# Two transformer blocks on one core: the FFNs' middle layers and u moved within 64 bytes

## The chip, the core and the metric

The kernel runs on one core of a Trainium2 chip. The metric is the device time of one execution in microseconds (us); of several executions the median is taken. The engines are TensorE (PE; its weight loads have a row of their own, PEld), VectorE (DVE), ScalarE (ACT), GpSimd (POOL) and SyncE (SP), which here issues the loads of the weights.

## The reference

Two blocks in a row on 256 tokens of 1024 features, in float32. The first block is an FFN, a mixer (gated linear attention and block attention), and an FFN; the second is the same frame twice (layers 1 and 2) with another mixer. Each FFN has a middle layer of 2816 features:

```
def swiglu(x, w_gate, w_up, w_down):
    return (jax.nn.silu(x @ w_gate) * (x @ w_up)) @ w_down

first block:   h = h + FFN_RES * g1 * swiglu(u, w_ff1_gate, w_ff1_up, w_ff1_down)   # u: normalised h
               h = h + g2 * token_mixing(u, w_in, ...)
               h = h + FFN_RES * g3 * swiglu(u, w_ff2_gate, w_ff2_up, w_ff2_down)
second block:  for l in range(2): the same order with swiglu_2 and concat(conv, hgrn2, fox) mixers
```

So there are six FFNs, numbered 0 to 5, and three mixers, numbered 0 to 2.

## The kernel before

Features lie on the 128 partitions and tokens along the free dimension, so a tile is 128 features by 256 tokens. u (the normalised input of a projection) has KD = 8 such tiles, an FFN's middle layer KF = 22. Float32 products are made of three matmuls in a rounded format: the weights and the moving operand are each split into a high and a low part (whi, wlo; uhi, ulo; hhi, hlo; mix_hi, mix_lo), and `three` (line 1749) issues high by high, high weights by low, low weights by high, each with 128 x 128 weights and a moving operand of 128 x 256. One such group is called a triple here.

Stages follow in this order: up0, down0, in0, branch, out0, up1, down1, up2, down2, in1, out1, up3, down3, up4, down4, in2, out2, up5, down5. An up projection has 22 chunks of weights, each of two halves (gate and up) by 8 tiles k: 352 triples, 1056 matmuls (`feature_tiles`, `first_tiles` for the chunk that waits for u). A down projection has 16 chunks of 11 tiles of the middle layer: 176 triples, 528 matmuls (`down` in TensorE's `ffn`). Chunks come by DMA into `raw`, a ring of 4 slots. ScalarE rounds a chunk into whi (line 750), VectorE subtracts into wlo (lines 1064 and 1073), and TensorE waits for wlo (`chunk_in`). PSUM banks alternate. The order of the work is written out by hand, with semaphores between engines.

Beside that, ScalarE writes a tile of uhi (line 798, or 777 for up0 and part of in0), VectorE writes ulo (lines 1099, 1115); ScalarE writes a tile of hhi (lines 819 and 829), VectorE writes hlo from it (line 1307).

Where the operands stand, in bytes along a partition. Tensors are placed one behind the other in the order in which they are declared, rounded up to 32 bytes. In the built program whi begins at 49280, wlo at 82048, ulo at 131200, uhi_room at 139392, mix_lo at 151808, hhi_room and merged_a at 180864, mix_hi at 184960 and merged_b at 203392: all are multiples of 64. hlo_room begins at 203424, 32 bytes past a multiple of 64. The slots of whi and wlo are 8192 bytes apart, weights within a slot step by 512 bytes, and tiles of the moving operands by 1024 bytes, so every tile of an operand has its first tile's place within 64 bytes, with one exception. `ahead = 8` elements of 4 bytes put uhi and hhi 32 bytes into their rooms:

```
        ahead = 8
        uhi_room = sb("uhi_room", [P, ahead + KD * (T + 2)], F32R)
        uhi = uhi_room[:, ahead:ahead + KD * T].rearrange("p (k t) -> p k t", t=T)
        uhi_shift = uhi_room[:, ahead:].rearrange("p (k t) -> p k t", t=T + 2)
```

The exception is uhi_shift, used in up1 and in the first two chunks of in0 (`shift_tiles`, `shift_three`, `second_of_in0`). There the high part has 258 columns per tile, two more than the 256 tokens, and tiles step by 1032 bytes, so tile k stands 32 + 8k bytes past a multiple of 64. In `second_of_in0` each k serves two triples in a row. In in0 from its third chunk on, and in in1 and in2, `token_tiles` uses the parts of u as the weights for some chunks and whi, wlo as the moving operand.

hhi_room and hlo_room share their bytes with tensors of the mixers (lv, aq, ak, av, gat and others down to cross). hidden_end only reserves the end of that overlap; prob and prob_t stand behind it.

Of the kernel before, what the change touches and what calls it, by code (L numbers as in the profile page):

```python
# [23 lines left out]
P = 128  # L24
T = 256
# [33 lines left out]
IN_CHUNKS = [GLA_CHUNKS, MIX_CHUNKS, MIX_CHUNKS]  # L59
ATT_HEADS = [4, 8, 8]  # L60
# [108 lines left out]
def build(nc, a, out):  # L169
    with ExitStack() as ctx:  # L170
# [21 lines left out]
        uhi = uhi_room[:, ahead:ahead + KD * T].rearrange("p (k t) -> p k t", t=T)  # L192
        uhi_shift = uhi_room[:, ahead:].rearrange("p (k t) -> p k t", t=T + 2)
        uhi_shifted = uhi_shift[:, :, 0:T]
# [71 lines left out]
        hhi_room = hidden.enter_context(nc.sbuf_tensor("hhi_room", [P, ahead + KF * T], F32R))  # L266
        hlo_room = hidden.enter_context(nc.sbuf_tensor("hlo_room", [P, KF * T], F32R))
        hhi = hhi_room[:, ahead:].rearrange("p (k t) -> p k t", t=T)
        hlo = hlo_room[:].rearrange("p (k t) -> p k t", t=T)
# [24 lines left out]
        sb("hidden_end", [P, 2 * KF])  # L294
# [447 lines left out]
        def _(act):  # L742
# [65 lines left out]
            def ffn(i):  # L808
                n0, e0 = seg(f"up{i}")

                def step(t, it=0):
                    dst = tiles_of(hhi, t, it, RING)
# [28 lines left out]
                def down(t):  # L841
                    split_ahead(n0 + t)
                    if t % 2 and name:
                        if g is not None:
                            if i == 0 and t == 1:
                                act.wait_ge(mods, 2)
                            gained_hi(g, e0 + t // 2, t // 2, into=uhi if i else uhi_shifted)
                        else:
                            act.wait_ge(evacuated, 2 + e0 + t // 2 + 1)
# [54 lines left out]
            def mixer(m):  # L904
# [100 lines left out]
                for t in range(4):  # L1005
# [3 lines left out]
                    for k in (2 * t, 2 * t + 1):  # L1009
                        gained_hi(g, e0 + t, k, into=uhi if m else uhi_shifted)  # L1010
# [47 lines left out]
        def _(dve):  # L1058
# [212 lines left out]
            def ffn(i, first_scale=None):  # L1271
                n0, e0 = seg(f"up{i}")

                def step(t, it=0):
# [32 lines left out]
                    nc.vector.tensor_tensor(tiles_of(hlo, t, it, RING), src, tiles_of(hhi, t, it, RING).bitcast(F32),  # L1307
# [35 lines left out]
                def down(t, it=0):  # L1343
# [4 lines left out]
                    else:  # L1348
# [16 lines left out]
                        if after is not None:  # L1365
                            gained_lo(SPLITS.index(FOLLOWS[f"down{i}"]), after, m, it, 2, uhi if i else uhi_shifted)
# [193 lines left out]
            def mixer(m):  # L1560
# [110 lines left out]
                for t in range(4):  # L1671
# [12 lines left out]
                    for k in (2 * t, 2 * t + 1):  # L1684
                        gained_lo(SPLITS.index(FOLLOWS[f"out{m}"]), next_gain(f"out{m}"), k, hi=uhi if m else uhi_shifted)
# [60 lines left out]
        def _(pe):  # L1746
# [14 lines left out]
            def feature_tiles(n, dst, tiles, width, kt):  # L1761

                vh, vl = kview(whi, n % RING, KD, width), kview(wlo, n % RING, KD, width)
                for j in tiles:
                    c = slice(j * P, (j + 1) * P)
                    for k in range(kt):
                        ins = three(dst[:, j * T:(j + 1) * T], vh[:, k, c], vl[:, k, c], uhi[:, k], ulo[:, k],
# [3 lines left out]
            def first_tiles(n, dst, waits, parted=(KD - 2, None)):  # L1771
# [3 lines left out]
                for ks in (range(at), range(at, KD)):  # L1775
                    if between and ks[0]:
                        between()
                    for j in range(2):
                        c = slice(j * P, (j + 1) * P)
                        for k in ks:  # L1780
                            if j == 0:
                                pe.wait_ge(ulo_ready, waits + k + 1)
                            ins = three(dst[:, j * T:(j + 1) * T], vh[:, k, c], vl[:, k, c], uhi[:, k], ulo[:, k],
# [136 lines left out]
            def ffn(i, stats=None):  # L1920

                n0, e0 = seg(f"up{i}")
                waits = KD * SPLITS.index(f"up{i}")

# [364 lines left out]
```

## Time and profile before

| | |
|---|---|
| time, median of 3 runs | 1637.3 us (1635.99 to 1637.68) |
| the profiled execution: its own time | 1638.61 us |
| its span | 1636.9 us |
| mean granted clock of TensorE | 0.999 |
| matmuls in the trace | 13617 |
| bytes read from HBM | 313.04 MB, 192 GB/s over the span |

The span runs from the first to the last instruction. The granted clock is a share of 2.4 GHz: 1.00 is the upper level and 0.50 the lower, 1.2 GHz. A matmul's displayed duration overlaps with that of the next ones, and so does a weight load's. How fast they follow each other is read from their starts, or from how many there are in a window. In a window that is filled from end to end, PE busy equals its length. The count in a window holds each instruction of which any part falls into it.

### The profile page before, as it was taken

To read this page: it belongs to the slowest core of one execution; us is meant where nothing else is said; L and a number is where in the kernel's file an instruction comes from. 1 tells how busy PE (TensorE), PEld (TensorE's weight loads), DVE (VectorE), ACT (ScalarE), POOL (GpSimd) and SP (SyncE) were. 2 spreads that over 40 slices of the span, in tenths; PEclk is the share of its full clock that TensorE was granted. 3 is DMA by queue.
4 is the path that set the end of the run, shared out by engine and by line. 5 is a ranking of instruction groups with operands and counts; after the bars stand their busy time and mean duration, and the time that the engine had idled before them with its cause. 6 is when DMAs were issued, how large, how long until landed. Compare 5 with 4: busy or idle time off the path is not lost.

```text
span 1636.9 us, 33817 instructions
## 1 busy us (share of the span) xinstructions
PE 1613.2 (99%) x13617; PEld 1575.4 (96%) x13617; DVE 1154.4 (71%) x1452; ACT 800.5 (49%) x973; POOL 171.6 (10%) x193
## 2 busy tenths in 40 slices
PE   6999999999999999999999999999999999999999
PEld 4999999999999999999999999999999999999999
DVE  6877789778766657666688876656665588776653
ACT  3444445355544455444464654445444465564442
POOL 1100114500000000000052200000000035200000
PEclk9999999999999999999999999999999999999999
DMA  9998797645766477655744566568664764456653
GB/s 332 312 313 248 243 333 228 219 153 182 183 188 187 133 196 205 193 165 159 230 140 130 146 179 189 150 178 218 192 189 142 209 190 130 129 157 190 177 160 114
DMA packets 501553, 315.62 MB, mean 193 GB/s; under 512 B 14815, under 2 KB 489674, under 8 KB 501450
## 3 DMA queue, kind: packets, MB, share of 16 engines
q1 hardware_dynamic: 491824, 282.33, 60.4%
q0 software_dynamic: 8496, 29.92, 5.2%
q8 instruction: 76, 1.25, 0.3%
q10 hardware_dynamic: 1130, 1.90, 0.3%
q14 instruction: 27, 0.22, 0.0%
HBM read 313.04 MB, written 1.05 MB: 192 GB/s over the span
## 4 chain that ended last, share of the span: by engine, by line
PE 71%; DVE 4%; ACT 2%; issue 1%; ACTq 0%; DVEq 0%
PE accs L1751 20%; PE accs L1753 20%; PE accs L1752 19%; PE accs L1789 1%; PE wide L1789 1%; PE wide L1791 1%; PE accs L1791 1%; PE wide L1790 1%; PE accs L1790 1%; DVE wlo L1064 1%; PE wide L2022 1%; PE accs L1849 1%; PE accs L1850 0%; PE accs L1851 0%; PE ps_score L2071 0%
## 5 line engine op out<-in xcount | busy, mean ns | idle before, releaser
L1751 PE MATMUL accs<-uhi_room,whi 128*128 128x256 f32 x2304 | 651.7, 283 | 3.0 <-DVE ulo L1115 1.2
L1753 PE MATMUL accs<-uhi_room,wlo 128*128 128x256 f32 x2304 | 646.4, 281 | 0.0
L1752 PE MATMUL accs<-ulo,whi 128*128 128x256 f32 x2304 | 644.3, 280 | 0.0
L750 ACT CAST whi<-raw 128x2048 fp32r<-128x2048 f32 (+2 forms) x294 | 500.5, 1705 | 107.1 <-PE accs L1753 60.7
L1064 DVE TENSOR_TENSOR wlo<-raw,whi 128x2048 fp32r<-128x2048 f32 (+2 forms) x249 | 496.5, 2002 | 4.5 <-ACT gat L991 3.1
L1751 PEld LDWEIGHTS accs<-uhi_room,whi 128*128 128x128 f32 x2304 | 435.6, 189 | 11.4 <-issue 5.2
L1752 PEld LDWEIGHTS accs<-ulo,whi 128*128 128x128 f32 x2304 | 432.1, 188 | 1.2 <-issue 1.2
L1753 PEld LDWEIGHTS accs<-uhi_room,wlo 128*128 128x128 f32 x2304 | 433.1, 188 | 0.0
L1751 PE MATMUL accs<-hhi_room,whi 128*128 128x256 f32 x1056 | 296.3, 281 | 0.8 <-DVE wlo L1064 0.8
L1752 PE MATMUL accs<-hlo_room,whi 128*128 128x256 f32 x1056 | 295.2, 280 | 0.0
L1753 PE MATMUL accs<-hhi_room,wlo 128*128 128x256 f32 x1056 | 294.4, 279 | 0.0
L1751 PEld LDWEIGHTS accs<-hhi_room,whi 128*128 128x128 f32 x1056 | 198.4, 188 | 2.0 <-issue 1.7
L1753 PEld LDWEIGHTS accs<-hhi_room,wlo 128*128 128x128 f32 x1056 | 198.5, 188 | 0.0
L1752 PEld LDWEIGHTS accs<-hlo_room,whi 128*128 128x128 f32 x1056 | 198.5, 188 | 0.0
L824 ACT ACTIVATE work<-work 128x256 f32<-128x256 f32 x88 | 37.0, 420 | 217.7 <-DVE work L1293 217.7
L1293 DVE TENSOR_TENSOR work<-accs,rstd 128x512 f32<-128x512 f32 x99 | 68.4, 691 | 103.7 <-PE accs L1753 103.5
L1073 DVE TENSOR_TENSOR wlo<-raw,whi 128x1024 fp32r<-128x1024 f32 (+1 forms) x90 | 116.2, 1296 | 0.5
L1307 DVE TENSOR_TENSOR hlo_room<-work,hhi_room 128x256 f32 (+1 forms) x132 | 56.2, 425 | 84.9 <-ACT hhi_room L829 77.8
L1363 DVE SCALAR_TENSOR_TENSOR h<-accs,half,h 128x256 f32 (+1 forms) x48 | 23.2, 484 | 114.3 <-PE accs L1753 114.3
L829 ACT CAST hhi_room<-work 128x256 f32 (+1 forms) x110 | 44.8, 407 | 42.7 <-DVE work L1303 35.1
L639 POOL DMA_DIRECT2D in_turn<-in_w_ada x56 | 30.3, 541 | 272.8 <-DVE intra L1240 153.8
L798 ACT ACTIVATE uhi_room<-h,vec_b 128x256 fp32r<-128x256 f32 x40 | 19.6, 509 | 79.3 <-DVE h L1363 66.3
(368 smaller groups left out, 2263.8 us busy)
## 6 DMA issues: line engine op xcount, KB each, us to landing
raw<-in_ffn_w_in SPq DMA_DIRECT2D x176, 512.0 KB, 5.0
in_turn<-in_w_ada POOLq DMA_DIRECT2D x56, 512.0 KB, 5.6
raw<-in_w_mix_in SPq DMA_DIRECT2D x52, 512.0 KB, 4.6
raw<-in_ffn_w_out SPq DMA_DIRECT2D x64, 384.0 KB, 3.6
raw<-in_w_ff_gate SPq DMA_DIRECT2D x44, 512.0 KB, 5.0
raw<-in_w_ff_up SPq DMA_DIRECT2D x44, 512.0 KB, 6.2
raw<-in_w_in SPq DMA_DIRECT2D x40, 512.0 KB, 5.1
raw<-in_ffn_w_out SPq DMA_DIRECT2D x64, 320.0 KB, 4.0
```

What stands on the lines that cost most here:

```text
L750: nc.scalar.copy(whi[:, n % RING, 0:cols], raw[:, n % RING, 0:cols]).then_inc(hi_ready, 1)
L824: nc.scalar.activation(pair[:, 0], pair[:, 0], ACT.Silu, bias=ws[:, t % 2, 0:1] if i == 1 else 0.0).then_inc(silu_ready, 1)
L829: nc.scalar.copy(dst, pair[:, 1]).then_inc(hhi_ready, 1)
L1064: nc.vector.tensor_tensor(wlo[:, n % RING, 0:cols], raw[:, n % RING, 0:cols], whi[:, n % RING, 0:cols].bitcast(F32), ALU.subtract).then_in ...
L1073: ins = nc.vector.tensor_tensor(wlo[:, n % RING, c], raw[:, n % RING, c], whi[:, n % RING, c].bitcast(F32), ALU.subtract)
L1293: nc.vector.tensor_tensor(pair, ps, by_token(2), ALU.mult).then_inc(evacuated, 1)
L1307: nc.vector.tensor_tensor(tiles_of(hlo, t, it, RING), src, tiles_of(hhi, t, it, RING).bitcast(F32), ALU.subtract).then_inc(hlo_ready, 1)
L1751: mm(dst, wh, xh, start=first, stop=False)
L1752: mm(dst, wh, xl, start=False, stop=False)
L1753: return mm(dst, wl, xh, start=False, stop=last)
L1789: mm(dst, wh, uhi_shift[:, k], start=first, stop=False)
L1790: mm(dst[:, 0:T], wh, ulo[:, k], start=False, stop=False)
```

## The change

Each of the six FFNs gets a place of its own for its middle layer, for hhi and hlo alike: `MIDDLE_FROM` elements into the rooms, which are 16, 48, 40, 24, 56 and 8 bytes for FFN 0 to 5. hhi_room is larger, so that hlo_room begins at 203648, now a multiple of 64. uhi begins at 16, 48, 40 and 24 bytes for up2, up3, up4 and up5, and stays at 32 for up0, in1, in2 and the later chunks of in0; up1 and the first chunks of in0 keep uhi_shift. ulo stays. The order of the instructions on each engine is the same, and so are their number and shapes; the parameters that carry the tiles (`xh`, `hhi[i]`) only choose addresses. prob and prob_t stand 128 bytes further up.

```diff
 IN_CHUNKS = [GLA_CHUNKS, MIX_CHUNKS, MIX_CHUNKS]
+MIDDLE_FROM = [4, 12, 10, 6, 14, 2]
 ATT_HEADS = [4, 8, 8]
...
         uhi_room = sb("uhi_room", [P, ahead + KD * (T + 2)], F32R)
-        uhi = uhi_room[:, ahead:ahead + KD * T].rearrange("p (k t) -> p k t", t=T)
+        def uhi_from(c):
+            return uhi_room[:, c:c + KD * T].rearrange("p (k t) -> p k t", t=T)
+
+        uhi = uhi_from(ahead)
         uhi_shift = uhi_room[:, ahead:].rearrange("p (k t) -> p k t", t=T + 2)
-        uhi_shifted = uhi_shift[:, :, 0:T]
+        uhi_of = {"in0": uhi_shift[:, :, 0:T], "up1": uhi_shift[:, :, 0:T], "up2": uhi_from(4), "in1": uhi, "up3": uhi_from(12),
+                  "up4": uhi_from(10), "in2": uhi, "up5": uhi_from(6)}
         work = sb("work", [P, 4, T])
...
         hidden = ExitStack()
-        hhi_room = hidden.enter_context(nc.sbuf_tensor("hhi_room", [P, ahead + KF * T], F32R))
-        hlo_room = hidden.enter_context(nc.sbuf_tensor("hlo_room", [P, KF * T], F32R))
-        hhi = hhi_room[:, ahead:].rearrange("p (k t) -> p k t", t=T)
-        hlo = hlo_room[:].rearrange("p (k t) -> p k t", t=T)
+        hhi_room = hidden.enter_context(nc.sbuf_tensor("hhi_room", [P, KF * T + 8 * ahead], F32R))
+        hlo_room = hidden.enter_context(nc.sbuf_tensor("hlo_room", [P, KF * T + 2 * ahead], F32R))
+        hhi, hlo = [[room[:, c:c + KF * T].rearrange("p (k t) -> p k t", t=T) for c in MIDDLE_FROM]
+                    for room in (hhi_room, hlo_room)]
         hidden.close()
...
         cross = sb("cross", [P, 4, P])
-        sb("hidden_end", [P, 2 * KF])
+        sb("hidden_end", [P, 80])
         prob = sb("prob", [P, 384])
...
                 def step(t, it=0):
-                    dst = tiles_of(hhi, t, it, RING)
+                    dst = tiles_of(hhi[i], t, it, RING)
                     if i == 0:
...
                                 act.wait_ge(mods, 2)
-                            gained_hi(g, e0 + t // 2, t // 2, into=uhi if i else uhi_shifted)
+                            gained_hi(g, e0 + t // 2, t // 2, into=uhi_of[FOLLOWS[f"down{i}"]])
                         else:
...
                     for k in (2 * t, 2 * t + 1):
-                        gained_hi(g, e0 + t, k, into=uhi if m else uhi_shifted)
+                        gained_hi(g, e0 + t, k, into=uhi_of[FOLLOWS[f"out{m}"]])
                     square_pair(["up1", "up3", "up5"][m], t)
...
                     src = hid[:, t % 2] if i == 0 else gate_up[:, t % 2, 1]
-                    nc.vector.tensor_tensor(tiles_of(hlo, t, it, RING), src, tiles_of(hhi, t, it, RING).bitcast(F32),
+                    nc.vector.tensor_tensor(tiles_of(hlo[i], t, it, RING), src, tiles_of(hhi[i], t, it, RING).bitcast(F32),
                                             ALU.subtract).then_inc(hlo_ready, 1)
...
                         if after is not None:
-                            gained_lo(SPLITS.index(FOLLOWS[f"down{i}"]), after, m, it, 2, uhi if i else uhi_shifted)
+                            gained_lo(SPLITS.index(FOLLOWS[f"down{i}"]), after, m, it, 2, uhi_of[FOLLOWS[f"down{i}"]])
                         split_ahead(n0 + t, it)
...
                     for k in (2 * t, 2 * t + 1):
-                        gained_lo(SPLITS.index(FOLLOWS[f"out{m}"]), next_gain(f"out{m}"), k, hi=uhi if m else uhi_shifted)
+                        gained_lo(SPLITS.index(FOLLOWS[f"out{m}"]), next_gain(f"out{m}"), k, hi=uhi_of[FOLLOWS[f"out{m}"]])
                     if t == 0 and m:
...
-            def feature_tiles(n, dst, tiles, width, kt):
+            def feature_tiles(n, dst, tiles, width, kt, xh=uhi):
                     for k in range(kt):
-                        ins = three(dst[:, j * T:(j + 1) * T], vh[:, k, c], vl[:, k, c], uhi[:, k], ulo[:, k],
+                        ins = three(dst[:, j * T:(j + 1) * T], vh[:, k, c], vl[:, k, c], xh[:, k], ulo[:, k],
                                     k == 0, k == kt - 1)
-            def first_tiles(n, dst, waits, parted=(KD - 2, None)):
+            def first_tiles(n, dst, waits, parted=(KD - 2, None), xh=uhi):
...
                                 pe.wait_ge(ulo_ready, waits + k + 1)
-                            ins = three(dst[:, j * T:(j + 1) * T], vh[:, k, c], vl[:, k, c], uhi[:, k], ulo[:, k],
+                            ins = three(dst[:, j * T:(j + 1) * T], vh[:, k, c], vl[:, k, c], xh[:, k], ulo[:, k],
                                         j == 0 and k == 0, j == 1 and k == KD - 1)
...
                 waits = KD * SPLITS.index(f"up{i}")
+                xh = uhi_of[f"up{i}"] if i else uhi
...
                     elif t == 0 and isinstance(it, int):
-                        ins = first_tiles(n0, acc[e0 % 2], waits, (4, second_part) if i == 0 else (KD - 2, None))
+                        ins = first_tiles(n0, acc[e0 % 2], waits, (4, second_part) if i == 0 else (KD - 2, None), xh)
                     elif i == 0 and t == 1 and isinstance(it, int):
                     else:
-                        ins = feature_tiles(n0 + t, acc[(e0 + t) % 2], range(2), 2 * P, KD)
+                        ins = feature_tiles(n0 + t, acc[(e0 + t) % 2], range(2), 2 * P, KD, xh)
                     ins.then_inc(chunk_used, 1)
...
                         kk = side * (KF // 2) + k
-                        ins = three(acc[(e0 + m) % 2][:, 0:T], vh[:, k], vl[:, k], hhi[:, kk], hlo[:, kk],
+                        ins = three(acc[(e0 + m) % 2][:, 0:T], vh[:, k], vl[:, k], hhi[i][:, kk], hlo[i][:, kk],
                                     kk == 0, kk == KF - 1)
```

## Rows read from the trace of the kernel before

**Rows 1.** The page: busy time of each engine, and the chain's shares by engine.

```profile
PE 1613.2 (99%) x13617; PEld 1575.4 (96%) x13617; DVE 1154.4 (71%) x1452; ACT 800.5 (49%) x973; POOL 171.6 (10%) x193
...
PE 71%; DVE 4%; ACT 2%; issue 1%; ACTq 0%; DVEq 0%
```

**Rows 2.** Matmuls in order of time, out0: start us, length us, engine, line.

```profile
412.00 0.28 PE L1751 MATMUL accs<-merged_a,whi 128*128 128x256 f32 x1
...
415.36 0.28 PE L1752 MATMUL accs<-merged_b,whi 128*128 128x256 f32 x1
```

**Rows 3.** Stretches: window, length, PE busy (matmuls), clock, DMA share, GB/s.

```profile
648.00:738.00 90.00, 90.00 (x766) 1.00 0.65 182
172.00:187.00 15.00, 15.00 (x131) 1.00 0.62 191
216.00:234.00 18.00, 18.00 (x155) 1.00 0.93 311
574.00:614.00 40.00, 40.00 (x345) 1.00 0.70 195
764.00:804.00 40.00, 40.00 (x342) 1.00 0.70 202
1080.00:1120.00 40.00, 40.00 (x342) 1.00 0.69 198
1268.00:1308.00 40.00, 40.00 (x345) 1.00 0.71 205
450.00:540.00 90.00, 90.00 (x754) 1.00 0.67 182
```

**Rows 4.** The stretch of half clock in in0, as rows 3, and its matmuls: start, length.

```profile
249.00:249.80 0.80, 0.80 (x6) 0.50 1.11 356
...
248.70 0.42 PE L1789 MATMUL wide<-uhi_room,whi 128*128 128x258 f32 x1
...
249.77 0.42 PE L1791 MATMUL wide<-uhi_room,wlo 128*128 128x258 f32 x1
```

**Rows 5.** Matmuls in order of time, out2, same columns.

```profile
1430.82 0.28 PE L1751 MATMUL accs<-mix_hi,whi 128*128 128x256 f32 x1
...
1434.36 0.27 PE L1751 MATMUL accs<-mix_hi,whi 128*128 128x256 f32 x1
```

**Rows 6.** Matmuls in order of time, one tour of up1.

```profile
496.15 0.28 PE L1789 MATMUL wide<-uhi_room,whi 128*128 128x258 f32 x1
...
496.87 0.28 PE L1789 MATMUL wide<-uhi_room,whi 128*128 128x258 f32 x1
...
497.22 0.28 PE L1789 MATMUL wide<-uhi_room,whi 128*128 128x258 f32 x1
...
497.58 0.28 PE L1789 MATMUL wide<-uhi_room,whi 128*128 128x258 f32 x1
...
497.94 0.29 PE L1789 MATMUL wide<-uhi_room,whi 128*128 128x258 f32 x1
...
498.31 0.28 PE L1789 MATMUL wide<-uhi_room,whi 128*128 128x258 f32 x1
...
499.03 0.28 PE L1789 MATMUL wide<-uhi_room,whi 128*128 128x258 f32 x1
```

**Rows 7.** Matmuls in order of time, second chunk of in0.

```profile
254.61 0.28 PE L1789 MATMUL wide<-uhi_room,whi 128*128 128x258 f32 x1
...
256.03 0.28 PE L1789 MATMUL wide<-uhi_room,whi 128*128 128x258 f32 x1
```

**Rows 8.** Writes of uhi and hlo: count, ns least/median/most, first and last start.

```profile
L798 ACT ACTIVATE uhi_room<-h,vec_b x40: 495/511/514, 757.6 to 1447.9; 128x256 fp32r<-128x256 f32 x40
...
L798 ACT ACTIVATE uhi_room<-h,gain x16: 495/510/513, 179.6 to 434.4; 128x256 fp32r<-128x256 f32 x16
...
L829 ACT CAST hhi_room<-work x110: 397/407/410, 444.2 to 1572.7; 128x256 f32 x80, 128x256 fp32r<-128x256 f32 x30
...
L1307 DVE TENSOR_TENSOR hlo_room<-work,hhi_room x132: 416/426/427, 55.5 to 1573.1; 128x256 f32 x76, 128x256 fp32r<-128x256 f32 x56
```

## The prediction, made before the change was run

> **What bounds the kernel now.** I read the page's first part, then its chain of waits, then steady stretches one by one, single matmuls in order of time, and last the writes of the operands. The first part is to show that TensorE is occupied in 1613.2 of 1636.9 us at the full granted clock, VectorE in 71% [rows 1]. The chain says the same from the other end: 71% of what led to the last instruction is TensorE and only 4% VectorE [rows 1]. So what moves the time is the spacing of matmuls, not their displayed duration. Single matmuls are shown 0.28 us long [rows 2], which holds their time in the pipeline, and they overlap: in 90 us of the third FFN's up projection (up2) there are 766 of them [rows 3]. As each is shown some 280 ns long at a spacing near 118 ns, a window counts about 280 / 118 = 2.4 that began before it; 90 us / (766 - 2.4) = 117.9 ns. That is how I read a spacing from every row of group 3.
>
> For one stretch the granted clock was 0.50, which is 1.2 GHz: five matmuls from 248.70 to 249.77, 214 ns each, or 256 columns at 1.2 GHz to within 1 ns [rows 4]. At 2.4 GHz the same would be 107 ns, so at the full level some 11 ns per matmul are lost that are not lost at the half level. Nothing in the trace waits in these stretches (PE busy equals the window in every row of group 3), so the 11 ns lie inside TensorE, and the reads of the weights and of the moving operand are what is left. Addresses could matter there, and they are all that the change touches. That the reads are the cause is my guess; no row shows it.
>
> **What the spacings say about addresses.** All rooms start at multiples of 64 bytes except hlo_room, which starts 32 bytes behind one. So before the change the offsets within 64 bytes are: weights 0, ulo 0, uhi 32, hhi 32, hlo 32, merged_a, merged_b, mix_hi and mix_lo 0. From the rows:
> - uhi 32 with ulo 0 (up2 to up5): 90 / 763.6 = 117.9 ns [rows 3]; up3 to up5 count 766 or 767 in windows of the same length, so I use 117.8.
> - hhi 32 with hlo 32 (the down projections): 345 in 40 us gives 40 / 342.6 = 116.8, 342 gives 40 / 339.6 = 117.8 [rows 3]. Down1 and down4 run at 116.8 (and down5, whose window of 40 us counts 345 too), down2 and down3 at 117.8, with the very same addresses of the operands. Down0 begins at 15 / 128.6 = 116.6 and ends at 18 / 152.6 = 118.0. So there are two levels for one layout, 1.0 to 1.1 ns apart, and something other than the offset chooses.
> - merged, all at 0: 28 matmuls from 412.00 to 415.36, 120.0 ns [rows 2].
> - mix, all at 0 too: 30 matmuls from 1430.82 to 1434.36, 118.0 ns [rows 5]. So the offset within 64 bytes is not the whole story either: 0 gives 120.0 in one place and 118.0 in another.
> - up1, where uhi steps by 258 elements, so that its offset goes through 32, 40, 48, 56, 0, 8, 16, 24 as k rises: 90 / 751.6 = 119.7 ns [rows 3]; one tour of eight k, 24 matmuls from 496.15 to 499.03, 120.0 [rows 6]. Two of three matmuls have 258 columns here; two columns at 2.4 GHz are 0.8 ns, 0.6 on the mean. That leaves 119.2, or 1.4 ns above the fixed offset of 32.
> - the same layout in in0's second chunk, where two triples in a row have the same offset: 12 matmuls from 254.61 to 256.03 (offsets 8, 16, 16, 24), 118.3 ns [rows 7], 117.7 without the two columns. Here odd offsets cost nothing. So the 1.4 ns of up1 may belong to the change of offset at every k, not to the offsets.
>
> **The change part by part.** (1) Up projections 2 to 5: uhi goes from 32 to 16, 48, 40 and 24 bytes, ulo stays at 0. 4 x 1056 = 4224 matmuls. (2) Down projections: hhi and hlo go to 16, 48, 40, 24, 56 and 8 bytes, from 32 both. 6 x 528 = 3168 matmuls. hlo_room begins at a multiple of 64 bytes now, and lies 224 bytes further up. (3) Up0, in0, up1, in1, in2, out and branch keep their operands' addresses. (4) The instructions that write uhi, ulo, hhi and hlo write or read shifted addresses: cast 407 ns, VectorE's subtraction 426 ns [rows 8]. The 16 activations of line 798 that take their scale from gain write uhi for in0 and up1, all at the touring offsets, in 495 to 513 ns with a median of 510; the 40 that take it from vec_b write at 32 and have a median of 511 [rows 8], so a shifted write costs nothing, and VectorE and ScalarE have slack (busy in 71% and 49% of the span) to hide it if it did. If that cover were gone, the spread of the cast, 397 to 410 ns, times 22 tiles would be 0.3 us per FFN. (5) hidden_end grows, which moves prob and prob_t by 128 bytes, by whole blocks of 64. I take 0.
>
> No row of before shows parts (1) and (2) at a fixed offset of 16, 48, 40, 24, 56 or 8 for long. Bounds from the nearest rows: below, every triple at 116.7 as down4: up 4224 x 1.1 = 4.6 us, down2, down3 and half of down0 1320 x 1.1 = 1.5 us, 6.1 us gained. Above, every triple at 120.0 as merged: 4224 x 2.2 = 9.3 us, and down from a mean of 117.2 3168 x 2.8 = 8.9 us, 18.2 us lost. The nearest row is the chunk of in0 with held offsets, at 117.7: I take 117.8 for up, that is 0. For down I take the mean over the two levels, 117.2, as it is: 0. Sum 0 for the whole kernel. The profiled execution took 1638.6 us around its span of 1636.9; the three timed runs have a median of 1637.3, 1.3 below it, and the prediction is for such a median: 1637.3 us.
>
> The Trainium skill's page "SBUF — State Buffer", section "Specifications (TRN2)", says that SBUF has 16-byte cachelines and that each crossing to a new line costs a penalty. By that rule 40, 24, 56 and 8 bytes would be worse than 16, 32 and 48, since 1024 bytes then touch 65 lines. The held offsets of 8 and 24 in group 7 don't show it; I keep it as a rival below.
>
> **The rivals.** (A) Faster. If what costs is that the moving read and the weight read start in the same place of a block, any offset but 0 is free: hi at 32 gives 116.7 for two matmuls and ulo at 0 gives 120.0 for the third, mean 117.8, as measured in up; merged 120.0 fits, down4's 116.7 fits. Then down2, down3 and late down0 should have been at 116.7 too, and mix at 120.0: against it. With offsets that suit better than 32 both levels can fall: in up1 the triple at 48 is the shortest of the tour, 496.87 to 497.22 or 350 ns, with 258 columns [rows 6]. The bound below prices it: 1637.3 - 6.1 = 1631.2. It counts as faster from 3.3 us (0.2% of 1637, about the least that a measurement of this kernel tells from no change), that is 0.45 ns over 7392 matmuls.
> (B) Slower. 32 is half a block, the furthest from every boundary, and each other offset is nearer to one; up1's 119.2 is then the price of an average offset. 4224 x 1.4 = 5.9 and 3168 x 2.0 = 6.3 us: 12.2 us, 1649.5. If half of the groups pay, 1643.4. For it: the longest triple of the tour is the one at 8, 497.94 to 498.31 or 370 ns, behind 360 at 0 [rows 6]. Against it: group 7. It decides from 0.45 ns on the mean.
 Against it group 7 and up1's tour, where the odd multiples of 8 take 0.35 to 0.37 us like the even ones.
> (D) The layout does not do what it says, as writes at shifted places become slow enough to reach TensorE: with the spread of the cast, 13 ns, for each of 132 tiles all on the path that is 1.7 us, 1639.0.
>
> **How the numbers follow.** No change in sum (a few offsets better, a few worse, within 3.3 us): 0.44. A 0.24, B 0.23, C 0.06, D 0.03, of which D mostly stays within 0.2%. So faster 0.24, within 0.2% 0.45, slower 0.31. The likeliest case's own range is 1634 to 1640.6. Stretched towards A's end (1631) and to B's half case with room for some more (1646), leaving out B's full case and the tail above: 1631 to 1646.
>
> **What the changed profile would show.** The same windows over up2 to up5 and down0 to down5, shifted by what was won or lost: counts of 766 in 90 us and 342 to 345 in 40 us for no change; 774 and 345 for A; 757 and 338 for B. Under C down2 to down5 lose and down0, down1 do not. Up1, the in, out and branch stages are controls, to stay within 0.2 us each, in0 and all before it too. The busy times and groups of VectorE and ScalarE should stay within 1%. What makes the prediction wrong: a mean spacing that moves by more than 0.45 ns over the ten groups, in particular if a fixed offset of 16 or 48 locks at 120.0 as merged does, or below 116.

## The result: slower by 0.6%

| | before | changed |
|---|---|---|
| median of 5 runs | 1637.68 us (1635.99 to 1641.24) | 1646.81 us (1645.66 to 1648.48) |
| ratio | | 1.0057, 95% interval 1.0044 to 1.0069 |
| span of the profiled execution | 1636.9 us | 1644.0 us |

The prediction said 1637.3 us, 1631 to 1646, and gave "slower" 0.31. The change is slower, and the time lies 0.8 us above the range. The spans of the two traces differ by 7.0 us. The medians differ by 9.1 us, because the traced execution of the changed kernel (1645.66 us) lies 1.15 us under its median and that of before (1638.61 us) 0.93 us over its own. The kernel before, timed again beside the later kernels, mostly took 1635 to 1638 us at a mean granted clock of 1.000 and 1639.5 to 1642.5 at 0.998 or less, with medians from 1637.7 to 1640.1, so totals that differ by 2 us say little and the stage lengths decide.

The page of the changed kernel, engine by engine, and the shares of the chain (the work that ended last, followed back from the end), against [rows 1]:

```profile
PE 1620.0 (99%) x13617; PEld 1582.9 (96%) x13617; DVE 1154.4 (70%) x1452; ACT 799.7 (49%) x973; POOL 171.5 (10%) x193
...
PE 72%; DVE 4%; ACT 2%; issue 1%; ACTq 0%; DVEq 0%
```

VectorE and ScalarE do what they did (1154.4 and 799.7 us busy, against 1154.4 and 800.5); TensorE has 6.8 us more. The same steady stretches as [rows 3], shifted a little where the stages moved; columns as there:

```profile
650.00:740.00 90.00, 90.00 (x759) 1.00 0.63 177
963.00:1053.00 90.00, 90.00 (x767) 1.00 0.66 183
1150.00:1240.00 90.00, 90.00 (x762) 1.00 0.65 181
1468.00:1558.00 90.00, 90.00 (x757) 1.00 0.65 181
172.00:187.00 15.00, 15.00 (x130) 1.00 0.61 180
217.00:232.00 15.00, 15.00 (x129) 1.00 0.96 319
575.00:615.00 40.00, 40.00 (x340) 1.00 0.68 191
768.00:808.00 40.00, 40.00 (x338) 1.00 0.70 201
1082.00:1122.00 40.00, 40.00 (x335) 1.00 0.70 193
1272.00:1312.00 40.00, 40.00 (x341) 1.00 0.71 200
1588.00:1628.00 40.00, 40.00 (x343) 1.00 0.57 161
450.00:540.00 90.00, 90.00 (x754) 1.00 0.66 181
```

The first four are up2 to up5. Up2 counts 759 matmuls in 90 us, not 766: 118.9 ns instead of 117.9. Up3 counts 767 as before, up4 762, up5 757. The down projections count 335 to 343 in 40 us, against 342 to 345. Down3, now at 24 bytes, is the worst at 335, which is 120.0 ns; down0's two windows give 117.6 and 118.5 ns. Up1, the last row, counts 754 in both. The clock is 1.00 in all rows. PE busy equals the window in all, but as each matmul is shown some 280 ns long, a short wait would not show in it. The starts in the traces tell more: there is one gap of 203 ns in the window at 172 and one in that at 1588, with 202 ns at the same places before, and no gap over 135 ns in the other rows.

By stage, from the start of a stage's first matmul to that of the next stage's (us), and the mean distance of successive starts in it (ns, gaps over 160 ns left out), worked out from the two traces:

| stage, its offset in bytes | before | changed | ns before | ns changed |
|---|---|---|---|---|
| down0, 32 to 16 | 67.36 | 67.13 | 116.9 | 118.2 |
| down1, 32 to 48 | 62.83 | 63.59 | 116.7 | 118.4 |
| up2, uhi 32 to 16 | 126.76 | 127.76 | 117.8 | 118.9 |
| down2, 32 to 40 | 62.18 | 62.99 | 117.8 | 119.3 |
| up3, uhi 32 to 48 | 125.27 | 125.27 | 117.8 | 117.8 |
| down3, 32 to 24 | 62.18 | 63.37 | 117.8 | 120.0 |
| up4, uhi 32 to 40 | 125.25 | 126.02 | 117.8 | 118.5 |
| down4, 32 to 56 | 61.64 | 62.30 | 116.8 | 118.0 |
| up5, uhi 32 to 24 | 125.28 | 126.81 | 117.8 | 119.2 |
| down5, 32 to 8 | 61.44 | 62.03 | 116.6 | 117.7 |
| up0, up1, branch, out0 to out2, in1, in2 | | | the same | the same to 0.1 |

The ups lose 3.3 us, the downs 3.8. Down0's slower matmuls don't show in its length, as it waited less. In0 behind it is 0.5 us shorter and the stretch ahead of up0 0.5 longer. In0 says nothing about the offsets: in the eight kernels with the same places in in0 (before, changed, and six below) it took 147.4 to 149.0 us. The stages of the last row kept their lengths within 0.02 us. An entry of the table is a mean over a stage, and a stage can change its spacing on the way: down0 before stood at 116.6 or so until its middle and at 117.8 from there on. The writes of the operands, as in [rows 8]:

```profile
L803 ACT ACTIVATE uhi_room<-h,vec_b x40: 492/511/517, 759.2 to 1452.8; 128x256 fp32r<-128x256 f32 x40
```
```profile
L834 ACT CAST hhi_room<-work x110: 394/407/409, 443.9 to 1579.1; 128x256 f32 x80, 128x256 fp32r<-128x256 f32 x30
```

The medians are 511 and 407 ns, as before.

### The profile page after: what moved, and what is told of

Read it like the earlier page. It is cut to its first block, busy times and chain, and to the rows that moved or that the text cites. A ratio compares the mean times of both kernels' runs of the same rounds, so it can differ in the third digit from the quotient of the medians.

```text
span 1644.0 us, 33772 instructions
## 1 busy us (share of the span) xinstructions
PE 1620.0 (99%) x13617; PEld 1582.9 (96%) x13617; DVE 1154.4 (70%) x1452; ACT 799.7 (49%) x973; POOL 171.5 (10%) x193
## 4 chain that ended last, share of the span: by engine, by line
PE 72%; DVE 4%; ACT 2%; issue 1%; ACTq 0%; DVEq 0%
PE accs L1756 20%; PE accs L1758 20%; PE accs L1757 19%; PE accs L1794 1%; PE wide L1794 1%; PE wide L1796 1%; PE accs L1796 1%; PE wide L1795 1%; PE accs L1795 1%; DVE wlo L1069 1%; PE wide L2028 1%; PE accs L1854 1%; PE accs L1855 0%; PE accs L1856 0%; PE ps_score L2077 0%
## 5 line engine op out<-in xcount | busy, mean ns | idle before, releaser
L1368 DVE SCALAR_TENSOR_TENSOR h<-accs,half,h 128x256 f32 (+1 forms) x48 | 23.2, 484 | 118.8 <-PE accs L1758 118.7
```

## The experiments

"Distance" below is how many bytes an operand starts behind the place of the weights, within 256 bytes. Spacings are means of successive starts as in the table, unless a row is named.

**Which part costs.** First the two halves of the change apart. Only the middle layers moved:

```diff
-        uhi_of = {... "up2": uhi_from(4), ... "up3": uhi_from(12), "up4": uhi_from(10), ... "up5": uhi_from(6)}
+        uhi_of = {... "up2": uhi_from(8), ... "up3": uhi_from(8), "up4": uhi_from(8), ... "up5": uhi_from(8)}
```

> Only the middle layers are moved (hhi and hlo at 16, 48, 40, 24, 56, 8 bytes, hlo_room 224 bytes up); uhi stays at 32 in every up projection. Theory (each stage has its own price, set by its own operands' addresses, and nothing else changes): up2 to up5 return to 126.8, 125.3, 125.3 and 125.3 us, the down projections stay as changed, 63.6, 63.0, 63.4, 62.3, 62.0 for down1 to down5, and the time is 3.3 us under the changed kernel's, 3.8 over the kernel before. Rival (the levels pass on from stage to stage): the downs change as well when the ups before them do.

Measured: 1642.19 us, ratio to before 1.0026 (1.0014 to 1.0038). In order up2, up3, down2, down3:

```profile
650.00:740.00 90.00, 90.00 (x766) 1.00 0.65 180
963.00:1053.00 90.00, 90.00 (x767) 1.00 0.64 180
768.00:808.00 40.00, 40.00 (x337) 1.00 0.71 205
1082.00:1122.00 40.00, 40.00 (x336) 1.00 0.68 191
```

The ups are back at 766 and 767, the downs at 337 and 336. Down1, down2, down3 take 63.60, 62.98, 63.37 us, as in the changed kernel to 0.01 us, and down5 62.02; down4 took 62.42, not 62.30.

Only u moved, rooms and middle layers as before:

```diff
-MIDDLE_FROM = [4, 12, 10, 6, 14, 2]
+MIDDLE_FROM = [8, 8, 8, 8, 8, 8]      # no longer read: hhi and hlo and their rooms as in the kernel before
```

> Only u is moved (uhi at 16, 48, 40, 24 bytes in up2 to up5); the middle layers and their rooms are as before. Own-price theory: up2 +1.0, up3 0.0, up4 +0.8, up5 +1.5 us, the downs as before (62.8, 62.2, 62.2, 61.6, 61.4 for down1 to down5), in all +3.3 us over before. Rival (levels pass on): the downs behind a changed up get another of the two levels seen before, 61.6 or 62.2 us.

Measured: 1641.42 us, 1.0016 (1.0005 to 1.0027). The same four windows:

```profile
650.00:740.00 90.00, 90.00 (x759) 1.00 0.64 179
963.00:1053.00 90.00, 90.00 (x762) 1.00 0.65 182
768.00:808.00 40.00, 40.00 (x345) 1.00 0.72 208
1082.00:1122.00 40.00, 40.00 (x345) 1.00 0.71 199
```

Up2 759 as in the changed kernel; up3 took 125.99 us here (762, 118.5 ns), where the changed kernel took 125.27 with the same addresses. So 48 has two levels as 32 has, 117.8 and 118.5. The downs were all at 345 (116.7 ns), down2 and down3 too. A stage has its own price, but which of its levels it gets differs between executions of nearly the same program.

**Offset or distance between the parts.** The change also put hlo_room 224 bytes further up. With the rooms of the changed kernel and 8 elements ahead everywhere, and with the changed offsets in one room that keeps hlo 22528 bytes behind hhi:

```diff
-        hhi_room = ...; hlo_room = ...
+        both_room = hidden.enter_context(nc.sbuf_tensor("both_room", [P, 2 * KF * T + 2 * ahead], F32R))
+        hhi, hlo = [[both_room[:, s + c:s + c + KF * T].rearrange("p (k t) -> p k t", t=T) for c in MIDDLE_FROM]
+                    for s in (0, KF * T)]
```

> The rooms are as changed, but every middle layer starts 8 elements (32 bytes) into them, so within 64 bytes all is as before and only the distance from hhi to hlo grows from 22528 to 22784 bytes, from 44 times 512 to 44.5 times 512. u as before. Theory O (the offset within 64 bytes is what costs): the downs are at 116.7 or 117.8 ns per matmul, as before. Theory D (the distance between the high and the low part, or to the weights, by more than 64 bytes is what costs): the downs are 1.2 to 2.2 ns slower, about 0.6 to 1.2 us each, 3.8 us in all.

> The middle layers start at 16, 48, 40, 24, 56 and 8 bytes past a multiple of 64 as changed, but hhi and hlo lie in one room 22528 bytes apart, as before. u as before. Theory O: the downs cost as in the changed kernel, 3.8 us over before. Theory D: they are as before. If both matter, both this one and the one with only the rooms changed lose a part.

Measured: rooms only 1638.58 us, 1.0004 (0.9994 to 1.0014), down1 to down5 63.34, 62.19, 61.68, 62.19, 61.44 us, at 117.7 or 116.7 ns; that is before's pair of levels. Offsets only 1642.58 us, 1.0030 (1.0019 to 1.0041), down1 to down4 63.59, 62.99, 63.37, 62.42 us. Down2 and down3 with the rooms only, then with the offsets only:

```profile
768.00:808.00 40.00, 40.00 (x342) 1.00 0.71 206
1082.00:1122.00 40.00, 40.00 (x345) 1.00 0.72 200
```
```profile
768.00:808.00 40.00, 40.00 (x338) 1.00 0.70 202
1082.00:1122.00 40.00, 40.00 (x336) 1.00 0.68 191
```

342 and 345 against 338 and 336: the offset costs, and 256 bytes more between the two parts do not. Other distances between them come further down. Down5, at 8 bytes, took 63.02 us (119.6 ns) here and 62.02 in the kernel with only the middle layers moved: so 8 has more than one level. By the starts, the first 12 of its 16 chunks stood at 120.0 ns here and at 117.7 there.

**Does the price belong to the offset?** The same offsets dealt to other FFNs:

```diff
-MIDDLE_FROM = [4, 12, 10, 6, 14, 2]
+MIDDLE_FROM = [2, 14, 6, 10, 12, 4]       # and uhi_from(6), (10), (12), (4) for up2 to up5
```

> The changed kernel with its offsets dealt to other FFNs: hhi and hlo at 8, 56, 24, 40, 48, 16 bytes for FFN 0 to 5, uhi at 24, 40, 48, 16 for up2 to up5. Theory (the price belongs to the offset): down2 at 24 and down3 at 40 swap their 120.0 and 119.3 ns, down4 at 48 takes 118.4, down1 at 56 118.0 to 118.2; up2 at 24 takes 119.2, up3 at 40 118.5, up4 at 48 117.8 or 118.5, up5 at 16 118.9. Rival (the price belongs to the place in the program): each stage keeps the figure of the changed kernel.

Measured, one execution: 1646.05 us. Down2 and down3:

```profile
768.00:808.00 40.00, 40.00 (x336) 1.00 0.69 197
1082.00:1122.00 40.00, 40.00 (x338) 1.00 0.68 188
```

They swapped: 24 bytes gives 120.0 ns wherever it is, 40 gives 119.3; 48 gave 118.3 in down4, 56 118.2 in down1, 16 118.4 in down5. Up2 at 24 took 119.3, up3 at 40 118.5, up4 at 48 117.8. Up5 at 16 took 118.5, not 118.9.

**All at zero.**

```diff
-MIDDLE_FROM = [4, 12, 10, 6, 14, 2]
+MIDDLE_FROM = [0, 0, 0, 0, 0, 0]          # and uhi_from(0) for up2 to up5
```

> The changed kernel with every offset at 0: hhi, hlo and the uhi of up2 to up5 at multiples of 64, like the weights. Theory (0 collides with the weights): 120.0 ns as in out0, ups 127.6 instead of 125.3 us, downs 63.4 instead of 61.6 to 62.2, in all 15 us or more over the kernel before, more than the changed kernel loses. Rival (mix operands stand at 0 and run at 117.8 ns): ups and downs at 117.8, within 2 us of before.

Measured: 1654.28 us, 1.0088 (1.0073 to 1.0104). Up2 and down2, 752 in 90 us and 336 in 40, both 120.0 ns:

```profile
650.00:740.00 90.00, 90.00 (x752) 1.00 0.63 176
768.00:808.00 40.00, 40.00 (x336) 1.00 0.68 197
```

So 32 was indeed better than 0, and mix at 117.8 with offsets of 0 within 64 bytes had to have another reason.

**Relative to what, and with which period.** Two kernels that move more than the change did. The first puts ulo 32 bytes up in a room 64 bytes larger, which moves all that lies behind by 64, hhi and hlo and merged among it. The second moves whi and wlo by 32 and all behind them by 64:

```diff
-        ulo = sb("ulo", [P, KD, T], F32R)
+        ulo_room = sb("ulo_room", [P, KD * T + 16], F32R)
+        ulo = ulo_room[:, 8:8 + KD * T].rearrange("p (k t) -> p k t", t=T)
```

```diff
+        sb("weights_ahead", [P, 8])
         whi = sb("whi", [P, RING, SLOT], F32R)
         wlo = sb("wlo", [P, RING, SLOT], F32R)
+        sb("weights_behind", [P, 8])
```

> The kernel before, but ulo too stands 32 bytes past a multiple of 64 (its room is 64 bytes larger; what is behind it moves by 64). Theory (a matmul whose moving operand is 32 bytes off the weights' place within 64 bytes takes 116.7 ns, with a second level at 117.8; at 0 it takes more): up2 to up5 go from 117.76 to between 116.7 and 117.8 ns, 0 to 1.1 us less each, the same in up0, and less in in0, in1, in2 and up1; in all 1 to 7 us under the kernel before. Rival (117.76 in the up projections is not ulo's price): no change beyond 0.3 us a stage, 1637 to 1638.

> The kernel before, but whi and wlo stand 32 bytes past multiples of 64 (8 elements ahead of them and 8 behind; all tensors behind keep their place within 64 bytes). Theory R (what counts is the place of the moving operand relative to the weights'): the downs and the high parts of the ups now start where the weights do and take 120.0 ns in the downs (63.4 us, 1.2 to 1.7 more each), while merged in out0 drops from 119.9 to 116.7 or 117.8 and its 23.68 us to 23.3 or less. Theory A (only the moving operand's own place counts): every stage keeps its time within 0.1 us, but for the downs' two levels, 61.6 and 62.2.

Measured: ulo moved 1647.79 us, 1.0051 (1.0037 to 1.0064); weights moved 1638.03 us, 0.9996 (0.9986 to 1.0007). First ulo, then weights: out0 in two pieces, down1, down2:

```profile
412.00:420.00 8.00, 8.00 (x73) 1.00 0.75 190
422.00:431.00 9.00, 9.00 (x78) 1.00 0.80 206
575.00:615.00 40.00, 40.00 (x336) 1.00 0.66 186
768.00:808.00 40.00, 40.00 (x336) 1.00 0.71 205
```
```profile
412.00:420.00 8.00, 8.00 (x70) 1.00 0.73 195
422.00:431.00 9.00, 9.00 (x80) 1.00 0.79 203
575.00:615.00 40.00, 40.00 (x342) 1.00 0.70 194
768.00:808.00 40.00, 40.00 (x342) 1.00 0.77 218
```

Neither theory foresaw the first: a move by 64 bytes, which leaves every place within 64 bytes as it was, took the downs to 120.0 ns. It took out0 from 120.0 [rows 2] to 113.3 for some 80 matmuls and, behind a wait, to 117.8 for the rest, by their starts (both at the same distance, 64 bytes, so two levels again). Up3 was at 119.9 there, the other ups from up2 on at 117.8 to 117.9. So the period is longer than 64 bytes. The pair tells what the place is relative to: hhi and hlo begin at bytes 180960 and 203488 in both kernels, and the downs take 120.0 ns with the weights at 49280, and 117.0 to 117.8 with the weights 32 bytes further. The 117.0 is a mean of two levels: in down1, 99 matmuls from 566.2 to 577.3 us, between two waits, stand 113.3 ns apart, and the rest some 117.8. So the operand's own address alone does not decide; I take the distance to the weights, which is 96 bytes in the first and 64 in the second, and test it again below. The expectation for the moved weights had the distance wrong (it forgot the 64 bytes by which the rest moved), so its numbers for the downs failed while its idea held. The longer period also offers a reason why mix differs from merged with all at 0 within 64: mix_lo lies 128 bytes from the weights' place within 256. No run moved mix_lo alone, so that is not shown; in the first sweep below, which moved mix_hi to 128 and mix_lo to 0, out1 went from 117.8 to 119.9 ns.

**Sweeps.** Since the price belongs to the offset, one execution can carry six in its downs and four in its ups. Three kernels did:

```diff
+MIDDLE_FROM = [56, 16, 48, 0, 8, 24]      # both_room behind a uhi_room 128 bytes larger; uhi_from(16), (32), (24), (48)
+MIDDLE_FROM = [44, 12, 4, 20, 36, 28]     # behind an ulo_room 64 bytes larger, ulo 16 in; uhi_from(0), (8), (16), (24)
+MIDDLE_FROM = [2, 6, 5, 3, 7, 1]          # behind u_room as shown further down; uhi_from(28), (30), (32), (36)
```

> Distances below are from the weights' place within 256 bytes. hhi and hlo lie 22528 bytes apart and stand 96, 192, 64, 128, 160 and 224 bytes behind the weights' place in FFN 0 to 5; uhi 64, 128, 96 and 192 in up2 to up5 with ulo at 0; merged and mix_hi at 128, mix_lo at 0. Theory 64 (only the place within 64 bytes counts): 64, 128 and 192 cost 120.0 ns like 0, and 96, 160, 224 cost 116.7 or 117.8 like 32. Theory 128 (the pattern repeats every 128 bytes): 128 costs 120.0 as 0, 192 as 64 (116.9 or 117.8 with the weights moved), 160 as 32 (116.7 or 117.8), 96 and 224 120.0 (as with ulo moved). Theory 256: 128, 160, 192 and 224 are free to differ from 0, 32, 64 and 96.

> Distances from the weights' place within 256 bytes as in the first sweep: hhi and hlo 240, 112, 80, 144, 208 and 176 bytes in FFN 0 to 5; ulo at 64, and uhi at 64, 96, 128 and 160 in up2 to up5. Theory 128: 144 costs as 16 (118.4 ns), 176 as 48 (118.4), 208 as 80, 240 as 112; in the ups 64/64 takes 116 to 117.8, 128/64 as a high part at 0. Theory 64: 80, 144 and 208 all as 16 (118.4), 112, 176 and 240 all as 48 (118.4), and 64/64 takes 120.0 as 0/0 did.

> Around 112: hhi and hlo at 104, 120, 116, 108, 124 and 100 bytes in FFN 0 to 5; ulo at 112 and uhi at 112, 120, 128 and 144 in up2 to up5. Theory (a smooth trough around 112): 108 and 116 within 1 ns of 113.5, 100 and 124 towards 118 to 120. Rival (steps of 16 bytes or a single point): all six at 116.7 or more, with 112/112 in up2 alone below.

Measured, one execution each: 1649.20, 1644.53 and 1638.00 us. All down projections of all kernels together, with hhi and hlo at the same distance (ns, means over a stage, which can mix two levels; two values where executions or stages differed by over 0.5):

| 0 | 8 | 16 | 24 | 32 | 40 | 48 | 56 | 64 | 80 | 96 |
|---|---|---|---|---|---|---|---|---|---|---|
| 120.0 | 117.7, 119.6 | 118.4 | 120.0 | 116.7, 117.8 | 119.3 | 118.4 | 118.1 | 117.0, 117.8 | 118.3, 120.0 | 120.0 |

| 100 | 104 | 108 | 112 | 116 | 120 | 124 | 128 | 144 | 160 | 176 | 192 | 208 | 224 | 240 |
|---|---|---|---|---|---|---|---|---|---|---|---|---|---|---|
| 120.3 | 119.6 | 120.0 | 113.5 to 114.4 | 121.7 | 120.2 | 119.9 | 118.7 | 118.4 | 118.7 | 119.0 | 117.8 | 119.2 | 118.1 | 117.0 |

The outlier is 112. Down1 of the second sweep, then down1, down2 and down4 of the third, at 120, 116 and 124:

```profile
575.00:605.00 30.00, 30.00 (x264) 1.00 0.67 187
```
```profile
571.00:611.00 40.00, 40.00 (x335) 1.00 0.67 186
760.00:800.00 40.00, 40.00 (x331) 1.00 0.69 199
1272.00:1312.00 40.00, 40.00 (x336) 1.00 0.73 214
```

264 in 30 us is 30 / (264 - 2.5) = 114.7 ns with a wait for weights in it; without it the starts are 113.5 apart. Four bytes to either side, 108 and 116, it is 120.0 and 121.7. There is no smooth trough, and the theory of one fell. Nor does a period of 128 hold: 128 is 118.7 where 0 is 120.0, and 224 is 118.1 where 96 is 120.0. These rest on one stage each at 128 and 224; the firmest pair is 240, at 117.0 here and 117.2 in a later kernel, where 112 is 113.5 to 114.4. In the ups (uhi/ulo): 64/0 118.9, 96/0 118.5, 128/0 119.9, 192/0 119.2, 64/64 and 96/64 117.8, 128/64 118.9, 160/64 118.3; 112/112 gave 113.4 ns, and 120, 128 and 144 over 112 gave 119.4, 118.3 and 117.8. Of the theories on the period, 64 falls with 64, 128 and 192 (117.8, 118.7, 117.8 and not 120.0), 128 with the two pairs named.

**Everything at 64, everything at 112.** The layout at 64 starts both_room and uhi_room at that distance and ulo 16 elements into its room. The layout at 112:

```diff
+        u_room = sb("u_room", [P, 28 + KD * T + KD * (T + 2)], F32R)
+        ulo = u_room[:, 28:28 + KD * T].rearrange("p (k t) -> p k t", t=T)
+        uhi = uhi_from(28)                # KD * T + 28 elements into u_room; uhi_shift starts there too
+MIDDLE_FROM = [4, 4, 4, 4, 4, 4]          # both_room stands 96 bytes behind the weights' place
```

> Everything that moves past the weights stands 64 bytes behind their place within 256: uhi (with its shifted form starting there), ulo, hhi, hlo, merged and mix_hi; mix_lo at 192. Theory (the distance to the weights sets the price, and 64 is the cheapest seen: 116.07 ns in out0 with ulo moved): ups 125.3 to 123.5 us, downs 61.4 to 61.7, out0 23.04, in all 6 to 10 us under the kernel before. Rival 64 (place within 64 bytes alone): as the kernel with all at 0, 120.0 ns, 15 us over before. Rival L (two levels as at 32): 117.8 ns in the ups, no gain there.

> uhi, ulo, hhi and hlo all stand 112 bytes behind the weights' place within 256 in every FFN (merged, mix_hi and mix_lo at 96). In the second sweep down1 ran at 113.52 ns there, with waits for weights between. Theory (the price belongs to the offset): the other downs follow, 113.5 to 117 ns, 60.0 to 61.8 us, and the ups, if the high and the low part at 112 do as in the downs, 113.5 ns or 120.7 us, 4.5 us less each; in all 10 to 25 us under the kernel before. Rival (113.5 is a rare second level of that one execution, as 116.7 beside 117.8): most stages at 117.8 or above, within 4 us of before.

Measured: at 64, 1636.29 us, 0.9987 (0.9978 to 0.9997); its ups from up2 on and most downs are at 117.8 ns as rival L said. Up1 takes 1.2 us less, in0 to in2 together 1.2 and out0 0.4, and the downs from down1 on 1.4 more. At 112, 1608.46 us, 0.9813 (0.9800 to 0.9826): 1.9% faster than before and faster than everything else here. The spans differ by 27.2 us and the medians by 30.0, more than the 10 to 25 us that were expected. Its page, then up2 to up5, down2 to down5 and up1:

```profile
PE 1581.8 (98%) x13617; PEld 1543.0 (96%) x13617; DVE 1154.6 (72%) x1452; ACT 800.6 (50%) x973; POOL 171.5 (11%) x193
```
```profile
640.00:730.00 90.00, 90.00 (x796) 1.00 0.69 192
950.00:1040.00 90.00, 90.00 (x797) 1.00 0.68 189
1140.00:1230.00 90.00, 90.00 (x796) 1.00 0.66 184
1440.00:1530.00 90.00, 90.00 (x797) 1.00 0.68 191
755.00:795.00 40.00, 40.00 (x352) 1.00 0.72 200
1060.00:1100.00 40.00, 40.00 (x349) 1.00 0.69 192
1240.00:1280.00 40.00, 40.00 (x349) 1.00 0.66 184
1560.00:1600.00 40.00, 40.00 (x355) 1.00 0.50 144
450.00:540.00 90.00, 90.00 (x751) 1.00 0.65 177
```

796 or 797 in 90 us, 113.4 ns, and 349 to 355 in 40 us. Single matmuls of down3, nine distances in 1.02 us, 113.3 ns:

```profile
1060.10 0.28 PE L1755 MATMUL accs<-both_room,whi 128*128 128x256 f32 x1
...
1061.12 0.28 PE L1755 MATMUL accs<-both_room,whi 128*128 128x256 f32 x1
```

Each up of 1056 matmuls takes 4.0 to 4.6 us less (up0 136.42, up5 120.76 us), in1 and in2 1.3 each. The downs take 0.5 to 1.7 less. Down0 takes 2.6 us more although its matmuls mostly stand 113.6 ns apart: its gaps over 160 ns exceed 118 ns each by 6.2 us in sum, 2.0 before. Half of that, 3.1 us, is a stretch of half clock from 204.9 to 211.7 us, with 31 matmuls mostly 213 ns apart; two waits of 1.3 us, at 193.6 and 202.4, stand ahead of it. In the trace of before down0 has no half clock. Up1, whose distance tours with k, is at 120.3 ns, 0.6 us more.

**Is it the distance at 112 too, and do both parts need it?**

```diff
+MIDDLE_FROM = [12, 20, 12, 20, 12, 20]    # weights moved by 32 bytes as above, one room
+MIDDLE_FROM = [(28, 28), (60, 60), (12, 28), (0, 28), (8, 28), (28, 60)]   # (hhi, hlo), weights as before
```

> whi and wlo stand 32 bytes past multiples of 64, hhi and hlo 22528 bytes apart. In FFN 0, 2 and 4 they start at byte 180976, exactly where they start in the kernel with all at 112, which is 80 bytes behind the weights' place now; in FFN 1, 3 and 5 at byte 181008, 112 behind the weights' place. Theory R (distance to the weights): down1, down3, down5 at 113.4 to 114.4 ns, 60 to 62.3 us, and down0, down2, down4 at 118.3 as 80 in the second sweep. Theory A (own address): the reverse.

> Weights as before; high/low part behind the weights' place: FFN 0 112/112, FFN 1 240/240, FFN 2 48/112, FFN 3 0/112, FFN 4 32/112, FFN 5 112/240. Theory P (the pattern repeats every 128 bytes in its main part): 240 and 112/240 take 113.4 to 114.4 like 112. Theory Q (it does not): 240 takes near 117 (down0 of the second sweep), and only down0 is at 113.5. For both: with the high part elsewhere the low part's 112 is worth little, 116 or more in down2, down3 and down4.

Measured, one execution each: 1636.73 and 1643.34 us. With the weights moved, down2, down3, down4 and down5:

```profile
768.00:808.00 40.00, 40.00 (x335) 1.00 0.72 209
1085.00:1115.00 30.00, 30.00 (x264) 1.00 0.73 203
1272.00:1312.00 40.00, 40.00 (x336) 1.00 0.72 208
1585.00:1615.00 30.00, 30.00 (x267) 1.00 0.66 182
```

Down2 and down4 start at the very byte at which all downs start in the kernel at 112, and count 335 and 336 in 40 us, 120.0 ns. Down3 and down5 start 32 bytes further, 112 behind the moved weights, and count 264 and 267 in 30 us, 113.9 and 113.6 ns. Theory R holds for 112, theory A falls. A remainder: 80 bytes gave 118.3 in the second sweep and 120.0 here. In the last kernel down0 (112 for both) was at 113.9 ns, down1 (240) 117.2, down2 (48 and 112) 117.8, down3 (0 and 112) 118.9, down4 (32 and 112) 117.8, down5 (112 and 240) 117.8. None of the four pairs with one part elsewhere reached 113.4 ns, so both parts have to be at 112, and 240 is not its equal.

## Why the prediction was wrong

- **What bounds, and where the change acts: right.** TensorE's spacing without waits was the quantity. Writes, VectorE, ScalarE, prob and the larger rooms cost nothing: up1, in1, in2, the out stages and branch stayed within 0.02 us where 0.2 was allowed; in0 moved by 0.5.
- **The step that failed: "I take 117.8 for up, that is 0. For down I take the mean over the two levels, 117.2, as it is: 0."** For up it rested on twelve matmuls of in0 [rows 7] and let them outweigh the 352 triples of up1 [rows 3]. Twelve matmuls 2.6 us behind a stretch of half clock [rows 4], with waits between, are not a steady stream, and the rows show starts to 10 ns only: by the starts in the trace they stand 118.6 ns apart, not 118.3. For down no row stood behind it. Measured, the ups took 118.9, 117.8, 118.5 and 119.2 ns, a loss of 3.3 us where the sum had 0, and the downs 117.7 to 120.0, a loss of 3.8 us where it had 0.
- **How far it was off.** The loss of 7.1 us over the stages, put on the 1637.3 us, would be 1644.4, inside the stated range. The median lies 2.4 us above that; the executions of the changed kernel spread over 2.8 us at a granted clock of 1.000 in all, and what sets that spread is not known.
- **Two readings of the rows were too fine or too trusting.** In the tour of up1 [rows 6] the starts in the trace give 359, 357, 354, 357, 365, 362, 360 and 359 ns for the offsets from 32 on. So the longest triple is the one at 0, with 365, and not the one at 8, with 362; that fits the 120.0 ns of the kernel with all at zero. And "Nothing in the trace waits in these stretches" was read from PE busy, which hid the gap of 202 ns in down0's first window.
- **The period of 64 bytes was an assumption**, and the rows had a warning in them that the text passed over: mix and merged both stand at 0 within 64 and differ by 2 ns [rows 2, 5]. Distances to the weights within 256 bytes put the two apart (mix_lo at 128).
- **Rival B had the direction and the size, but not the reason.** It said 1.4 ns in the ups and 2.0 in the downs if every group pays, 12.2 us, and 6.1 us if half do. Measured were 0 to 1.5 and 1.1 to 2.2 ns, 7.1 us. Its ground, that 32 is the furthest from a boundary, is not borne out: 56 and, at one of its levels, 8 are among the cheaper, 24 is the dearest of the six. Its chance of 0.23 was low, and the upper end of 1646 left out its full case.
- **Rival C** expected down2 to down5 to lose and down0, down1 not. Down0 and down1, at 16 and 48, lost 1.3 and 1.7 ns. The Trainium skill, "SBUF — State Buffer", section "Specifications (TRN2)", says that each cross to a new 16-byte line pays a penalty: by that rule 0, 16, 32 and 48 would be alike and 8, 24, 40 and 56 worse. In the downs 24 and 40 are dearer indeed (120.0 and 119.3 ns), but 56 is at 118.1 beside 118.4 for 16 and 48, and 0 is at 120.0. The rule does not order them.
- **Rival A** priced each distance but 0 as free. Its bound of 116.7 ns was also no bound: 113.4 exists. The prediction took the lowest spacing that it saw held in a stage as a floor, while half clock [rows 4] had shown that 107 is what the columns alone would need.

What stays open: why 112, what sets which of two levels a stretch gets, and why 80 gave two values. The spacing of 113.3 ns is not peculiar to 112, as 64 showed it too for some 80 and 99 matmuls behind a wait; what was seen at 112 alone is that it came in every stage with both parts there. That two reads inside TensorE collide would fit a price that follows the distance between the two operands, but no run looked inside a read, so it is argued and not shown. Whether the pattern repeats after 256 bytes was not tried; the kernel with the rooms alone moved put hlo 256 bytes further within 512 and stayed as before, which speaks for it as far as hlo goes.

## What to carry over

Where TensorE streams float32 parts with no waits, its spacing can depend by 7% (113.4 to 121.7 ns) on where the moving operand starts relative to the weights; sweep that distance in steps of 4 or 8 bytes over at least 256, high and low part together, with a different value in each stage, and then give all of them the best. Count matmuls in fixed windows, since busy shares and single durations hide this, and look at the starts within a window for a wait or a change of level. And when two places share a supposed cause but differ in spacing, the supposed cause is incomplete: take the cases as wide as the widest spacings seen in steady streams.

## What the hardware showed that was not expected

- At distance 112, 128 x 128 weights with 256 moving columns follow each other in 113.4 ns; at 108 and 116 in 120.0 and 121.7. Before was at 117.8.
- The same program text has two levels at some distances (116.7 and 117.8 at 32, 117.8 and 118.5 for uhi at 48, 117.7 and 120.0 at 8, 113.3 and 117.8 at 64), often kept through a whole stage and different between executions. It can change on the way: in the kernel with ulo moved, out0 went from 113.3 to 117.8 ns at a wait, in the one with the weights moved down1 went from 117.8 to 113.3 and back, at waits, and down0 before went from some 116.6 to 117.8, all with the operands' distances kept.
- The distance to the weights decides, not the moving operand's own address: at byte 180960, 120.0 or 117.0 to 117.8 ns; at byte 180976, 113.6 to 114.4 or 120.0.
